# Last block of a three-block transformer kernel: tile 0's norm and turns ahead of tile 1's copies and output products

## What is computed

```python
def second_block(x, c, ...):
        ...
        mixed = jnp.einsum('bse,ed->bsd', jnp.concatenate([attn, pool], axis=-1), w_out[l])
        x = x + g1 * mixed
        h2 = rmsnorm(x, norm2_g[l]) * (1.0 + sc2) + sh2
        x = x + g2 * peer_ffn(h2, peer_wq[l], peer_subkeys[l], peer_u[l], peer_v[l])
    return rmsnorm(x, final_g)

def peer_ffn(h, w_q, sub_keys, expert_u, expert_v):
        ...
        q = jnp.einsum('cd,de->ce', xc, w_q).astype(jnp.float32).reshape(C, PEER_HEADS, 2, half)
        s = jnp.einsum('chpk,pnk->chpn', q, sub_keys.astype(jnp.float32))
        sv, si = lax.top_k(s, K)
        ...
        top_v, top_pos = lax.top_k(cand, K)
        eid = jnp.take_along_axis(cand_id, top_pos, axis=-1)
        gate = jax.nn.softmax(top_v, axis=-1)
        u = expert_u[eid]
        act = jax.nn.gelu(jnp.einsum('cd,chkd->chk', xc, u).astype(jnp.float32), approximate=False)
        vv = expert_v[eid]
        y = jnp.einsum('chk,chkd->cd', (gate * act).astype(vv.dtype), vv)
```

## Time and profile before

| | us |
|---|---|
| median of 3 runs | 1442.89 |
| lowest and highest | 1441.75, 1445.24 |
| the profiled execution, its own time | 1441.95 |
| span of the profiled execution | 1440.2 |
| PE busy | 1285.7 (89%) |
| DVE busy | 813.4 (56%) |
| ACT busy | 412.5 (29%) |
| POOL busy | 640.2 (44%) |
| DMA queue q0, the gathers | 268.45 MB, 45.1% of 16 engines' span |

### The profile page before, as it was taken

The page is one execution under the profiler, slowest core; times in us unless marked ns, Lnnn a source line. Parts: engine busy times, 40 slices in busy tenths (PEclk is TensorE's granted clock), DMA queues, the critical chain, the costliest instruction groups (busy, mean ns, idle before and its releaser), DMA issues.

```text
span 1440.2 us, 17400 instructions
## 1 busy us (share of the span) xinstructions
PE 1285.7 (89%) x6248; PEld 791.2 (55%) x6248; DVE 813.4 (56%) x1681; ACT 412.5 (29%) x1032; POOL 640.2 (44%) x643
## 2 busy tenths in 40 slices
PE   9999999999999999999998989958968788687886
PEld 8877686547876686548656555523423233233332
DVE  0776287431566387431338766789797654454455
ACT  0533333201333333212223332332322232222123
POOL 0566667522446666513003434544644454444440
PEclk9999999999999999999999999988988999989999
DMA  9544344444444344445355999999999999999995
GB/s 376 191 162 176 118 164 170 177 178 176 174 163 175 118 188 185 174 156 202 130 221 218 413 415 416 420 419 420 419 421 420 420 420 420 421 420 420 420 420 213
DMA packets 53600, 407.82 MB, mean 283 GB/s; under 512 B 6133, under 2 KB 8586, under 8 KB 10890
## 3 DMA queue, kind: packets, MB, share of 16 engines
q0 software_dynamic: 36864, 268.45, 45.1%
q1 hardware_dynamic: 15562, 137.21, 24.8%
q10 hardware_dynamic: 1088, 1.05, 0.4%
HBM read 404.56 MB, written 1.07 MB: 282 GB/s over the span
## 4 chain that ended last, share of the span: by engine, by line
PE 57%; DMA 26%; DVE 8%; issue 4%; ACT 4%; POOL 1%; SPq 0%; ACTq 0%; POOLq 0%; DVEq 0%
PE pj L671 23%; PE pj L707 9%; DMA ring<-in_peer_uv,vM 9%; PE bank L1096 9%; PE pj L686 6%; DMA yT<-in_peer_uv,vM 5%; DMA hv<-in_peer_uv,vM 3%; DMA more_rows<-in_peer_uv,vM 3%; DMA qM<-in_peer_uv,vM 3%; PE pj L966 2%; DMA ring<-in_units 1%; PE bank L644 1%; PE bank L916 1%; PE bank L811 1%; DVE tri L1848 1%
## 5 line engine op out<-in xcount | busy, mean ns | idle before, releaser
L671 PE MATMUL pj<-xT,ring 128*128 128x256 f32 (+2 forms) x1536 | 325.6, 372 | 2.2 <-ACTq L1144 1.7
L671 PEld LDWEIGHTS pj<-xT,ring 128*128 128x128 f32 (+1 forms) x1536 | 278.2, 189 | 43.5 <-issue 3.6
L598 POOL TENSOR_SCALAR more_rows<-more_rows,lbt 128x256 f32<-128x256 f32 x168 | 172.6, 1028 | 16.4
L632 POOL DMA_INDIRECT ring<-in_peer_uv,vM x101 | 115.7, 1146 | 117.5 <-PE bank L1096 106.5
L596 POOL TENSOR_SCALAR mod_part<-more_rows,lbt 128x256 f32<-128x256 f32 x24 | 27.0, 1127 | 259.7 <-issue 121.3
L707 PE MATMUL pj<-ring,yT 128*128 128x512 f32 x320 | 140.4, 595 | 0.4 <-DMA ring<-in_units 0.4
L1314 ACT ACTIVATE rope<-vM 128x4 f32<-128x4 f32 (+3 forms) x84 | 17.1, 204 | 408.1 <-DVE big L1848 325.4
L599 POOL TENSOR_TENSOR mod_part<-mod_part,more_rows 128x256 f32<-128x256 f32 x168 | 127.6, 760 | 14.0
L1096 PE MATMUL bank<-ring,causal 128*128 128x512 f32 x200 | 97.3, 624 | 18.9 <-ACT causal L1322 18.9
L1096 PE MATMUL bank<-ring,tri 128*128 128x512 f32 x204 | 98.1, 620 | 13.3 <-ACT tri L1322 13.3
L707 PEld LDWEIGHTS pj<-ring,yT 128*128 128x128 f32 x320 | 59.8, 190 | 71.6 <-issue 71.5
(11 more groups left out here) (368 smaller groups left out, 2109.2 us busy)
## 6 DMA issues: line engine op xcount, KB each, us to landing
ring<-in_units SPq DMA_DIRECT2D x44, 2048.0 KB, 9.4
more_rows<-in_w_ada SPq DMA_DIRECT2D x24, 1024.0 KB, 4.9
ring<-in_units SPq DMA_DIRECT2D x2, 1536.0 KB, 6.6
ring<-in_peer_uv,vM POOLq DMA_INDIRECT x101, 18.9
memT<-in_mem SPq DMA_DIRECT2D x1, 1024.0 KB, 5.1
ring<-in_units SPq DMA_DIRECT2D x2, 512.0 KB, 6.3
ring<-in_units SPq DMA_DIRECT2D x1, 1024.0 KB, 8.8
xT<-in_x_turned SPq DMA_DIRECT2D x1, 1024.0 KB, 10.5
```

The source lines that it names most:

```text
L598: do(g.tensor_scalar(mod_w[:, c, :], mod_w[:, c, :], silu_c[:, c:c + 1], None, ALU.mult))
L632: pool.indirect_dma_start(row_slot[k], None, d["peer_uv_2"], bass.IndirectOffsetOnAxis(ap=expert[:, t, j:j + 1], axis=0))\
L671: ins = nc.tensor.matmul(pj[s][0:n, 2 * m + first:2 * m + stop], ring[:, slot, at:at + n], act[:, c, first:stop], start=(c == 0), stop=(c ...
```

## The change

The orders of PE, ACT and DVE in the last block are rewritten around tile 0's norm. On PE the turns Zt come behind P5, ahead of Y4 and Y5; K0at and E0t come ahead of tile 1's output products O1u, O0v and O0w; the product of pick 0 (W1) stands behind K0bt, and those of picks 1 and 2 (W3) behind Zu, ahead of K1at. On ACT half_norm is cut in two (OMta, OMtb), which lie around the copy P3, ahead of the copies P4 and P5. On DVE the norm and the scaling of tile 0 come ahead of Y5's copy, H2t and GT1 ahead of OMu, and H2u ahead of Zu. Four of the banks get fixed numbers (BANK_FIXED). Later tasks of the block move by a place or two.

```diff
-            """... P2 O0t P3 Y2 P4 Y3 P5 Y4
-            Y5 O1u Zt O0v K0at E0t O0w K0bt E1t K1at Zu K1bt E2t K0au W4 K0bu E3t W5 W7 EU0 K1au W11 ...
+            """... P2 O0t P3 Y2 P4 Y3 P5 Zt
+            Y4 Y5 K0at E0t O1u O0v O0w K0bt W1 E1t Zu W3 K1at W4 K1bt E2t K0au W6 E3t K0bu W8 EU0 K1au W11 ...
...
-ACT_LAST = """... S3 S4 P2 S5 P3 P4 P5 OMt Zt K0at E0t T1 K0bt E1t OMu Zu K1bt W1
-    E2t W5 E3t W7 K0bu W8 T2 W11 EU0 ...
+ACT_LAST = """... S3 S4 P2 S5 OMta P3 OMtb P4 P5 Zt K0at E0t T1 OMu K0bt W1
+    E1t Zu W4 K1bt E2t W6 E3t K0bu W8 T2 EU0 W11 ...
...
-DVE_LAST = """... N5 OMt Y5 NMt Zt Rt0 XP1 OMu H2t NMu D1 Zu D3 H2u D4 GT1
-    D5 Rt1 D8 XP2 D9 Rt2 ...
+DVE_LAST = """... N5 OMt NMt Zt Y5 Rt0 XP1 H2t GT1 OMu D1 NMu D2 H2u Zu
+    D4 Rt1 D7 XP2 D9 Rt2 ...
...
+BANK_FIXED = {("PT", 3): 1, ("AO", 1): 2, ("PT", 4): 0, ("PT", 5): 3}
...
+            if l == B2 and task == "Y2":
+                use((l, ("AO", 1)), BANK_FIXED["AO", 1])
             for key in bank_uses(l, task):
-                use((l, key), n % 2 if few else n % 4)
+                if l == B2 and key == ("AO", 1):
+                    out[l, key] = (n, *out[l, key][1:])
+                else:
+                    use((l, key), BANK_FIXED[key] if l == B2 and key in BANK_FIXED else n % 2 if few else n % 4)
...
-            def half_norm(t, ready, spare):
+            def half_norm(t, ready, spare, halves=range(2)):
...
-                for half in range(2):
+                for half in halves:
...
+                if halves[-1] == 0:
+                    return
...
-                    half_norm(t, "x_mid", pT_of if t else [flat_pair[:, 0:COLS], flat_pair[:, COLS:]])
+                    half_norm(t, "x_mid", pT_of if t else [flat_pair[:, 0:COLS], flat_pair[:, COLS:]],
+                              {"": range(2), "a": (0,), "b": (1,)}[task[3:]])
```

More of the change, by code:

```diff
@@ L65 @@
             L17 Y9 AD O0 LD L18 HO2 HO3 AD HN2 AD O2 LD HN3 O3t AD O1t O3u O1u""",
-            """Xt BUt Xu MT BUu BK BQa BQb SK S0 S1 BVa S2 PL0 PL1 BVb P0 P1 S3 S4 Y0 S5 Y1 O1t P2 O0t P3 Y2 P4 Y3 P5 Y4
-            Y5 O1u Zt O0v K0at E0t O0w K0bt E1t K1at Zu K1bt E2t K0au W4 K0bu E3t W5 W7 EU0 K1au W11 K1bu W15 EU1 W21
+            """Xt BUt Xu MT BUu BK BQa BQb SK S0 S1 BVa S2 PL0 PL1 BVb P0 P1 S3 S4 Y0 S5 Y1 O1t P2 O0t P3 Y2 P4 Y3 P5 Zt
+            Y4 Y5 K0at E0t O1u O0v O0w K0bt W1 E1t Zu W3 K1at W4 K1bt E2t K0au W6 E3t K0bu W8 EU0 K1au W11 K1bu W15 EU1 W21
             K20 W27 K21 W31 K22 W32 K23 W36 E4 W37 E5 W40 K30 W42 K31 W45 K32 W49 K33 W55 E6 E7 W256"""]
@@ L72 @@
     Le18 HO2 HN2 HO3 HN3 LN"""
-ACT_LAST = """Xu BU BK BQa BQb SK S0 S1 MT S2 BV P0 P1 S3 S4 P2 S5 P3 P4 P5 OMt Zt K0at E0t T1 K0bt E1t OMu Zu K1bt W1
-    E2t W5 E3t W7 K0bu W8 T2 W11 EU0 W18 K1bu W20 T3 W21 EU1 W35 K23 W38 E4 W39 E5 W51 T4 W57 K33 W61 E6 W62
+ACT_LAST = """Xu BU BK BQa BQb SK S0 S1 MT S2 BV P0 P1 S3 S4 P2 S5 OMta P3 OMtb P4 P5 Zt K0at E0t T1 OMu K0bt W1
+    E1t Zu W4 K1bt E2t W6 E3t K0bu W8 T2 EU0 W11 W18 K1bu W20 T3 W21 EU1 W35 K23 W38 E4 W39 E5 W51 T4 W57 K33 W61 E6 W62
     E7 W65 T5 W96 T6 W129 T7 W148 FN0 W256 FN1"""
@@ L79 @@
     Da15 Da16 S9 Da17 P9 Y7 Db15 Db16 L14 Y8 Db17 L15 L16 L17 AD Da18 Db18 L18 Y9 HO2 AD HO3 HN2 AD HN3 AD LN"""
-DVE_LAST = """Xu S0 S1 S2 PL0 PL1 N0 N1 S3 N2 S4 S5 N3 N4 Y1 N5 OMt Y5 NMt Zt Rt0 XP1 OMu H2t NMu D1 Zu D3 H2u D4 GT1
-    D5 Rt1 D8 XP2 D9 Rt2 D15 Rt3 D16 GT2 D18 XP3 D37 GT3 D44 Rt4 D50 Rt5 D54 XP4 D62 GT4 D63 Rt6 Rt7 D72 XP5
+DVE_LAST = """Xu S0 S1 S2 PL0 PL1 N0 N1 S3 N2 S4 S5 N3 N4 Y1 N5 OMt NMt Zt Y5 Rt0 XP1 H2t GT1 OMu D1 NMu D2 H2u Zu
+    D4 Rt1 D7 XP2 D9 Rt2 D15 Rt3 D16 GT2 D18 XP3 D37 GT3 D44 Rt4 D50 Rt5 D54 XP4 D62 GT4 D63 Rt6 Rt7 D72 XP5
     D77 GT5 Ru0 D81 Ru1 D83 Ru2 Ru3 D89 XP6 D104 GT6 D105 Ru4 D106 Ru5 D110 Ru6 D115 Ru7 D121 XP7 D137 GT7
```

## The result

| | before | after |
|---|---|---|
| median, us | 1442.64 (4 runs) | 1452.41 (4 runs) |
| lowest and highest | 1441.75, 1445.24 | 1448.18, 1454.45 |
| ratio, 95% interval | | 1.0070 (1.0049 to 1.0090) |
| profiled execution, span | 1441.95, 1440.2 | 1448.18, 1446.4 |
| first gather issued | 765.71 | 754.78 |

The forecast was 1446.0 (1438 to 1450), +3.6 us on the profiled execution. Measured: +6.2 us there and +9.8 us at the medians. I had given "slower" 0.36 and "same" 0.52.

A forecast was written before the change was run, and what follows sets the result against it. The bound was a full stream of expert gathers, paced from pick 18's landing. PE 7.9 us late, less a 4.7 us cushion, gave about +3.6 us on 1441.95: 1445.6, by the median 1446.5, stated as 1446 (range 1438 to 1450).

The forecast's parts named there:

- The head start: Last block, tile 0's scores ahead of tile 1's output products: first gather issued at 756.0 instead of 765.7, 9.7 us earlier.
- second wait: PE behind tile 1's turns: idle 6.7 us until ACT delivers the weights of picks 1 and 2 together.
- second product: PE's product of pick 1: claimed to start only at 780.0, behind 6.7 us of idle time.
- third wait: PE behind K0b's half: 1.9 us of waiting, since ACT has pick 6's weight behind K0's copy.
- The slow clock: PE's products after the first two waits run at the halved clock, costing 1.6 and 2.5 us.
- sums of 18.5 lost and 10.2 before: PE's idle and slow time up to K1's end: 18.5 us in the changed kernel, 10.2 in the old one.
- the cushion: Pick 18's gather stood in line 4.7 us, so PE could be that late before the stream feels it.
- fill the engines to 820: DMA engines ahead of pick 15: K3's load (5.0 us, issued 807.2) and picks 13 and 14 keep them busy until 820.
- the stream is full as before: Behind pick 18: gathers keep the old pace of about 2.5 us each, so nothing further is lost.
- +7 bound: Upper bound on the total change: first landing 1.5 us late and slow stretches longer by 2 us.
- Rival 1: The head start survives because PE doesn't open the slots: 1433.8 or about 1437, median 1436; chance 0.12.
- Rival 3: First landing late behind K1's 2.1 MB load, so PE's second gap grows: 1447 to 1450; chance 0.36.

The follow-up runs named there:

- e6: Changed kernel with PE's two waits filled by needless K1 products for tile 0, later overwritten; 1446.7 us, ratio 1.003 to the kernel before.
- e2: Changed kernel with the products of picks 0 to 7 back in their old places on PE and ACT, early scores kept; 1435.8 us.
- e14: e2 with 5.4 us of needless K1 products for tile 0 put behind Zu on PE; 1443.5 us, ratio 1.001 to the kernel before.
- e3: Changed kernel with K1's first half for tile 0 moved on PE ahead of the products of picks 1 and 2; 1447.2 us.
- e4: Kernel before with only tile 0's norm and turns moved ahead and fixed banks, tile 1's output products still ahead of K0; 1442.8 us.
- e8: e2 with picks 0 and 1 weighed singly and made early, picks 2 and 3 ahead of K0au, 4 and 5 ahead of K0bu; 1441.8 us.
- e9: e8 with ACT's order alone altered: weights of picks 2 and 3 ahead of head 2's copy, 4 to 6 ahead of head 3's; 1436.2 us.

## Why the prediction was wrong

**The head start** was right: forecast 9.7 us, measured 10.9 in the profiled execution and 9.8 as the mean of the four, each against the one profile of the kernel before.

**PE's schedule** was right to about 1 us. This execution's first gather was 1.2 us earlier than forecast, so its later times may be read as 1.2 us more. Forecast against measured: first product 768.0 and 767.1, second wait 6.7 and 6.9, second product 780.0 and 780.2, slow until 786.0 and 785.3, third wait 1.9 and 1.86, K1's last half over at 825.8 and 825.4, pick 18 issued at 826.1 and 825.8. The signs that I named as proof against me (second product by 775, last half by 820, a pace behind 830 that isn't 2.5 us) didn't come. The slow clock I took at 1.6 + 2.5 = 4.1 us; the rows give 4.4, e6 gives 3.1 by the distance and 5.5 by the ratios. My sums of 18.5 lost and 10.2 before came out at 19.8 and 10.6.

**The step that failed is the cushion**, the time that PE could be late by for nothing. I wrote "7.9 late, less 4.7, is 3.2": pick 18's gather had stood in line for 4.7 us in the old kernel, and I took these off. Its issue came 7.6 us later than in the old kernel. By the estimate above its landing came 4.7 us later (forecast 3.6), and the last dot 6.2. So 2.9 of the 4.7 us were had at pick 18, and 1.4 at the end. Two readings were wrong:
- **Up to pick 18's landing.** I let K3's load and picks 13 and 14 "fill the engines to 820". Pick 14's dot, which waited for its gather, started at 821.66, pick 17's at 830.77 where I had 829.7, though the issues of 13 to 18 were within 0.4 us of mine. The share was 0.96, but the rate 371 GB/s where it had been 419, which is 24 x 48 / 420 = 2.7 us of stream less than the kernel before carries from 808 to 832 us. In e2 K3's load lies in the stretch ahead (issued at 792.6), and both stretches run at 419 to 423. That the line was too short in the changed kernel fits this, but no run changes the length of the line alone.
- **Behind pick 18.** I wrote "the stream is full as before". It is fed by PE there too: the slots of K2 opened at 885.66 instead of 879.08, and the 20 us from 880 ran at 395 instead of 415 GB/s, about 1 of the 1.5 us that the last dot lost behind pick 18's landing.

Issue to last dot is 609.6 us before and 608.2 after, though the time in line ahead of pick 18 shrank by 2.9: half of it came back behind. The table says it more shortly: the rest of the program follows pick 18's issue by 607 to 610 us. In e14 the delay lies ahead of all the gathers that wait for PE, so it moved the whole stream; in the changed kernel the second wait, the longer one, lies ahead of all of them but gather 7.

**The profiled execution stood below the median by more than I took.** I carried over the 0.94 us between the old kernel's profiled execution and its median. The changed kernel's median is 4.2 us above its profiled execution. The miss at the medians, 6.4 us, is 2.6 of stream (the last dot at 1434.0 instead of 1431.4), 3.3 of this difference, and the 0.5 by which I rounded the forecast down. Of the 4.2 about 1.2 are the profiled execution's early start against the mean of the four profiles. In the altered kernels the profiled execution lies between 1.1 us above the median (e3) and 4.0 below it (e4). Where the changed kernel's other executions lose the remaining 3 us was not settled.

**The range.** Its upper end, 1450, was the +7 bound of the sum, and every term of that sum still had the cushion taken off. That PE's 7.9 us are paid in full was no case of mine, though it gives 1441.95 + 7.9 = 1449.9 for this execution and 1450.8 at the median, still 1.6 under the measured one. A saving that is read off one moment of a queue needed a bound of zero.

**The rivals.** Rival 1 (the head start survives if PE isn't the one that opens slots) comes nearest in e2, at 1435.8, where I had put it at 1436. But PE opens slots there as well (gather 7 is issued at 783.63, behind PE's product); it only waits less, so that the numbers meet is in part luck. The early products were what stood against it. Rival 3 (slower by more) was right in its direction only, since 1452.4 is beyond its 1450. Its way, a late first landing, did occur: K1's load was issued at 752.5, ahead of the first gather, and pick 0's dot started at 763.42, 8.6 us after its issue. But PE waited 4.24 us for it instead of 3.8, so it accounts for about 0.4 us.

## What to carry to other kernels

In a stage where one engine both works through a backlog and frees the slots of a stream, count that engine's idle and slow time ahead of the slots' opening nearly one for one to the end of the program (here 5.4 us put in gave 6.1 by the distance), and don't subtract what stands in line at one moment. A product that isn't ready must not stand ahead of work that is: put it behind as much ready work as its input needs, and look at the order on the engine that makes its input as well (e8 to e9: 6 us by the ratios, for two places on ACT). When an edit both brings a start forward and moves the work that follows, try the halves apart; here one was worth -7 us and the other +17.
